# Two transformer blocks in float32 on one NeuronCore: where a pair's transposes stand among the gate products

## The reference

```python
# per layer, x: 512 x 1024
h = rms_norm(x, attn_pre_gain)
u = h @ w_in          # q, k, v of two attentions, small gates, and g_a, g_b (1024 each)
# A: 8 heads of 64, window of 128, softmax with a sink
o_a = swa_sink_attention(qa, ka, va, sinks)
# B: 8 heads of 64, three softmaxes per head: 31 compressed keys, selected keys, window
o_b = gt0 * softmax(q_raw @ k_cmp) @ v_cmp \
    + gt1 * softmax(q_rot @ k_slc) @ v_slc + gt2 * softmax(q_rot @ k_win) @ v_win
mixed = sigmoid(g_a) * (o_a @ w_branch_a) + sigmoid(g_b) * (o_b @ w_branch_b)
x = x + rms_norm(mixed @ w_out, attn_post_gain)
# then a convolutional feed-forward network
```

## Time and profile before

| | |
|---|---|
| median of 3 runs | 4067.94 us (4066.13 to 4071.62) |
| profiled execution, its own time | 4067.59 us |
| span of that execution | 4065.7 us |
| mean granted TensorE clock | 0.925 |
| TensorE busy with matmuls | 3532.4 us, 87% of the span |
| VectorE busy | 2471.6 us, 61% |
| ScalarE busy | 1926.3 us, 47% |
| GpSimd busy | 207.3 us, 5% |
| TensorE's share of the chain that ended last | 81% (VectorE 9%, ScalarE 3%) |

### The profile page before, as it was taken

How to read it: one execution, slowest core, us unless ns; L and a number is a source line. 1 busy time by engine, 2 the same in 40 slices (tenths; PEclk the granted TensorE clock), 3 DMA queues, 4 the chain that set the end, 5 groups by cost and what they waited for, 6 DMA issues and landing times.

```text
span 4065.7 us, 54663 instructions
## 1 busy us (share of the span) xinstructions
PE 3532.4 (87%) x16820; PEld 2774.2 (68%) x16820; DVE 2471.6 (61%) x3734; ACT 1926.3 (47%) x2998; POOL 207.3 (5%) x253
## 2 busy tenths in 40 slices
PE   7999899989999899989877784999997886759995
PEld 5766588767767688767666664888886664548884
DVE  3677466433676466445555534899996336359995
ACT  3366433323465433333422222788885334338883
POOL 0000000000000000000000001111111000011110
PEclk9899999999899999989988895999998898869998
DMA  3211122222211122222100004999997110059994
GB/s 136 84 43 53 62 93 93 87 99 73 79 43 63 63 93 95 88 88 93 62 1 0 0 0 150 343 366 368 357 377 289 57 68 0 0 201 370 383 382 152
DMA packets 161993, 554.13 MB, mean 136 GB/s; under 512 B 28800, under 2 KB 28864, under 8 KB 160576
## 3 DMA queue, kind: packets, MB, share of 16 engines
q1 hardware_dynamic: 141760, 518.70, 35.2%
q0 software_dynamic: 16832, 16.90, 1.2%
q10 hardware_dynamic: 3264, 16.78, 1.1%
HBM read 555.40 MB, written 38.85 MB: 146 GB/s over the span
## 4 chain that ended last, share of the span: by engine, by line
PE 81%; DVE 9%; issue 4%; ACT 3%; DMA 1%; POOL 0%; ACTq 0%; DVEq 0%; POOLq 0%; SPq 0%
PE psum L605 22%; PE psum L607 21%; PE psum L606 21%; PE psum L642 3%; PE psum L832 2%; PE psum L711 2%; PE psum L744 1%; PE psum L945 1%; DVE arena L1884 1%; PE psum L726 1%; PE psum L673 1%; PE psum L1034 1%; PE psum L915 1%; DVE arena L1608 1%; DMA arena<-rows_out_m 1%
## 5 line engine op out<-in xcount | busy, mean ns | idle before, releaser
L2149 DVE TENSOR_TENSOR ew_r<-arena,ehigh_r 128x1024 fp32r<-128x1024 f32 x648 | 749.2, 1218 | 13.9 <-ACT ehigh_r L1444 13.9
L605 PE MATMUL psum<-oab_r,highs 128*128 128x512 f32 x1648 | 681.3, 413 | 54.2 <-DVE h_r L1601 17.5
L1586 DVE TENSOR_TENSOR ring_rounded<-ring,highs 128x1024 fp32r<-128x1024 f32 x302 | 368.4, 1221 | 541.6 <-ACT highs L1099 541.1
L607 PE MATMUL psum<-oab_r,ring_rounded 128*128 128x512 f32 x1648 | 648.2, 393 | 0.0
L1444 ACT ACTIVATE ehigh_r<-arena 128x1024 fp32r<-128x1024 f32 x648 | 631.0, 1053 | 0.0
L606 PE MATMUL psum<-h_r,highs 128*128 128x512 f32 x1296 | 509.7, 393 | 0.0
L1099 ACT ACTIVATE highs<-ring 128x1024 fp32r<-128x1024 f32 x302 | 318.8, 1057 | 346.5 <-PE psum L607 320.9
L605 PEld LDWEIGHTS psum<-oab_r,highs 128*128 128x128 f32 x1648 | 312.4, 190 | 159.1 <-DVE h_r L1601 38.3
L605 PE MATMUL psum<-ehigh_r,xT_high_r 128*128 128x512 f32 x864 | 352.7, 408 | 13.8 <-DVE ew_r L2149 7.6
L607 PEld LDWEIGHTS psum<-oab_r,ring_rounded 128*128 128x128 f32 x1648 | 311.6, 189 | 75.2
L607 PE MATMUL psum<-ehigh_r,xT_low_r 128*128 128x512 f32 x864 | 341.8, 396 | 0.0
(11 more groups left out here) (339 smaller groups left out, 6030.4 us busy)
## 6 DMA issues: line engine op xcount, KB each, us to landing
arena<-in_moe_w SPq DMA_DIRECT2D x648, 512.0 KB, 6.0
ring<-in_wstream SPq DMA_DIRECT2D x328, 512.0 KB, 3.3
rows_in_m<-arena ACTq DMA_DIRECT2D x4, 2048.0 KB, 9.0
arena<-rows_out_m ACTq DMA_DIRECT2D x8, 1024.0 KB, 5.5
x<-in_xT SPq DMA_DIRECT2D x1, 2048.0 KB, 11.5
result<-x SPq DMA_DIRECT2D x1, 2048.0 KB, 6.3
const<-in_const SPq DMA_DIRECT2D x1, 1004.0 KB, 5.0
arena<-rows_in_m,arena POOLq DMA_INDIRECT x58, 6.9
```

The costliest lines, as they stand in the source:

```text
L605: pe.matmul(acc, lhs[0], rhs[0], start=start, stop=False)
L607: return pe.matmul(acc, lhs[1], rhs[0], start=False, stop=stop)
L1586: dve.tensor_tensor(ring_r[:, c % R, :], ring[:, c % R, :], highs[:, c % HIGHS, :].bitcast(F32), ALU.subtract).then_inc(weights_split, seq ...
L2149: TT(ew_r[p], ew[:, p, :], ehigh_r[p].bitcast(F32), ALU.subtract).then_inc(expert_split[mi], 1)
```

## The change

In TensorE's loop over the pairs, `turn(p)` moves from between the two gate steps to the end of the pair, behind `weigh(p - 1)`. Nothing else is changed:

```diff
@@ -753,10 +753,10 @@
                     if p + 2 < NP:
                         scores(p + 2)
                     gate_step(2 * p)
-                    turn(p)
                     gate_step(2 * p + 1)
                     if p:
                         weigh(p - 1)
+                    turn(p)
                 weigh(NP - 1)
                 meet("branch")
                 for r in range(8):
```

## The result

| | before | changed |
|---|---|---|
| median | 4069.43 us (4 runs, 4066.13 to 4071.62) | 4115.04 us (4 runs, 4111.12 to 4116.75) |
| ratio to before | | 1.0111, 95% interval 1.0094 to 1.0129 |
| span of the profiled execution | 4065.7 us | 4114.9 us |
| mean granted clock | 0.925 | 0.923 |

The change costs 45.6 us, 1.1%; 4116.5 us was predicted.

The account below looks back on a forecast made before the run. The prediction took TensorE, busy throughout the heads' streams, as the bound. It added 24 us for a fourth passage, 21.5 for gate-bank waits and 3.5 for the stream ends, 49 us on 4067.59, predicting 4116.5 us, range 4094 to 4134.

Parts of the forecast that it names:

- Term 1: Transposes between value sums and scores add a fourth passage between kinds of weights on TensorE: 0.20 us in 120 pairs, 24 us.
- Term 2: Gate products wait for psum bank 7, emptied by ScalarE behind the later evictions: 30 waits in two layers, 21.5 us.
- Term 3: At each layer's stream end, later last transposes delay the branch products by 1.9 us: 3.8 us in two layers, net 3.5.
- rival C: The clock falls in the stream's longer waits, half speed after each of six: +15 us, 4131.6 us; chance 4%.
- Rival A: Faster: 128 gate products behind transposes lose a 0.09 us switching price, -11.5 us, 4055.8 us; chance 3%.
- Rival B: Transposes' or scores' weights load while the block before streams, so the fourth passage costs 0.10, 12 us: 4107.6 us; chance 20%.

Follow-up runs that it names:

- e3: Changed kernel with the gate bank emptied ahead of the eviction on ScalarE and each layer's last pair in the old order; 4087.01 us, ratio 1.0040 to the kernel before.
- e4: Kernel before with the value sums moved ahead of the transposes, between the two gate products; 4096.64 us, ratio 1.0063.
- e2: Changed kernel with the transposes behind both gate products but ahead of the value sums; 4074.36 us, ratio 1.0012 to the kernel before.
- e1: Changed kernel with ScalarE emptying the gate bank ahead of the eviction in every fourth pair; 4090.89 us, ratio 1.0053 to the kernel before.
- e5: Kernel before rewritten with two pairs per block, value sums and scores grouped in twos, ScalarE and VectorE orders to match; 4058.21 us, ratio 0.9972.
- e8: e5 with the first transposes ahead of the first gate product and ScalarE's second eviction ahead of the next exponentials; 4055.26 us, ratio 0.9963 to the kernel before.
- e9: e5 with only ScalarE's order changed, the second eviction ahead of the next exponentials; 4087.26 us, ratio 1.0042 to the kernel before.

## Why the prediction was right

The forecast case came, 4115.0 against 4116.5. Part of that closeness is luck: the forecast was 49 us on 4067.59, the measured difference is 45.6 on 4069.43, and two of its parts are off in opposite directions. Term by term:

- **Term 1**, the fourth passage, put at 0.20 us in 120 pairs, 24 us: the mechanism was right (e3, e4, and against it e2), the size too large. T between W and S is 0.15 dearer than its stream, as start distances show, 0.11 to 0.12 for the narrow transposes of cmp (205.85 to 206.18 is 0.33 for two), 17 us in all; e3 gives some 16. The step that was mis-sized is the late first matmul of T behind W, put at 0.10 as for G behind W: it is 0.05 to 0.06 late (227.60 to 227.76). The 0.10 for S behind T held, 0.09, and so did W to T at 0.15 in place of W to S.
- **Term 2**, the bank's wait, 21.5 us in 30 waits: 30 waits, 20.2 us, mostly of 0.48 and 1.33 us as idle time. By start distances, in which the prediction reckoned, they cost 0.55 and 1.40 where 0.55 and 1.39 were worked out, and one of 0.83 per layer brings the sum to 22.2. The added 0.10 for T's late first matmul was 0.05 at eight transposes (1.20 against 1.15), on the chain and on TensorE's own way alike, so it dropped out. e1 shows that the whole term goes with ScalarE's order.
- **Term 3**, the end, 1.9 us per layer: T(63) starts 2.58 us behind its pair's first G in place of 0.80, so 1.7 to 1.8. What I had not priced is the clock behind it, 2.5 and 2.0 us. I had looked for a fall of the clock (rival C) inside the stream; there it stayed at 1.00 through waits of 1.33 us. It fell behind the stream, where 1.19 and 2.20 us of idle time stand with only W(63), 1.1 us, between them. Whether that caused it is not shown.
- The excess of term 1, 7 us, and the 4.5 us of clock that were missing, stand on opposite sides; so the sum is nearer than its parts.
- G beside G gives nothing (210.46 to 210.70), and T between two G costs 0.11 per transpose, so there was nothing to give back. Rival A had no ground.
- Rival B, half a passage with 12 us, is the rule of the Trainium skill's TensorE: Matmul & The Clock Gate, The mechanism, that loads for a non-conflicting row group or for the background buffer are pulled ahead. Between G and T the trace agrees with it, with a load 0.23 us ahead of its matmul; at the borders with W and S the load starts with the matmul (227.59 and 227.60), so they are not pulled ahead there, and B's reason fails. Its size was not far off: 16 to 17 us lie between B's 12 and my 24, nearer to B.
- TensorEngine Tiling (Array Packing), Key Properties, of the Trainium skill, says "Mode switching requires drain". The trace agrees in that each border between these shapes costs time: 0.15 us for W to T to S, and 0.2 us saved where two S stand together. That it is a drain which costs it no run here shows.

## What to carry to other kernels

On a saturated TensorE, order the work so that matmuls of like shape in the array stand together, and price a move by start distances at each border, not by durations. Ask of each moved producer what stands behind its consumer in another engine's queue: here the gate bank was late because it was emptied behind an eviction that waits for the moved transposes. When two orders are coupled, batching can cost waits of its own: e5 gained 0.3%, and of the two further orders of ScalarE one gained a little more (e8) and one lost 0.4% (e9).

## What was not expected of the hardware

- The clock: behind 1.19 and 2.20 us of idle time with 1.1 us of work between them it was at 1.2 GHz for some 5 us in layer 0 (steps of 0.43 us), and for some 3 us in layer 1. Behind 1.98 us alone it stayed at 2.4 GHz in the kernel before, in both layers, and fell in e5, in both layers. Inside e9's stream it fell behind a wait of 0.83 us.
- Value sums over 31 rows and over 128 rows, both with 64 columns, do not count as alike: 0.59 us from one to the other, as to the scores. Sixteen and sixteen instructions of like value sums together take 1.90 us (220.67 to 222.57 in e5, from value sums to scores), 0.16 less than twice 1.03.
- Transposes with 31 columns of weights between two gate products cost no passage at all, 0.13 to 0.14 us from the first of two to the next product, as the full ones do (228.56 to 228.69 in the kernel before).
